# Second mixer's attention: the values of a step right behind its transposes, both parts of the main work behind them

## The reference, cut to what matters

```
z = rms_norm(x) @ w_in                      # all inputs of the three branches and their gates
o_a = fox_attention(q, k, v, f) * silu(..)  # 4 heads, causal, with a decay
o_b = conformer_conv(..) * silu(..)         # 31 taps, layer norm, a 256x256 product
o_c = nsa_attention(..) * silu(..)          # 8 heads: compressed + selected + window
x = x + concat(o_a, o_b, o_c) @ w_out
```

## Time and profile before

| what | value |
|---|---|
| median of 3 runs | 1589.8 us (1589.47 to 1591.67) |
| the profiled execution, its time | 1590.37 us |
| the profiled execution, its span | 1588.6 us |
| PE busy | 1574.3 us, 99% |
| DVE busy | 947.5 us, 60% |
| ACT busy | 800.6 us, 50% |
| POOL busy | 167.7 us, 11% |
| mean granted TensorE clock | 0.999 |

### The profile page before, as it was taken

The page is one execution under the profiler, slowest core; times in us unless marked ns, Lnnn a source line. Parts: engine busy times, 40 slices in busy tenths (PEclk is TensorE's granted clock), DMA queues, the critical chain, the costliest instruction groups (busy, mean ns, idle before and its releaser), DMA issues.

```text
span 1588.6 us, 22788 instructions
## 1 busy us (share of the span) xinstructions
PE 1574.3 (99%) x8752; PEld 1358.2 (86%) x8752; DVE 947.5 (60%) x1432; ACT 800.6 (50%) x1350; POOL 167.7 (11%) x187
## 2 busy tenths in 40 slices
PE   9999999999999999999999999999999999999998
PEld 7888899988888888888889988888888888889896
DVE  5555474544765554655456544575554679777876
ACT  6444465455464444544455545445444547553753
POOL 0000032211300000000011212131000201010110
PEclk9999999999999999999999999999999999999999
DMA  7555455333455554655545443446555473246321
GB/s 259 206 211 203 152 198 182 125 143 138 165 176 188 193 184 161 211 184 181 192 155 204 140 159 120 146 148 211 201 207 202 148 248 109 87 146 217 132 92 61
DMA packets 76142, 269.60 MB, mean 170 GB/s; under 512 B 8448, under 2 KB 9728, under 8 KB 76032
## 3 DMA queue, kind: packets, MB, share of 16 engines
q1 hardware_dynamic: 75744, 267.35, 47.6%
q10 hardware_dynamic: 288, 0.79, 0.1%
HBM read 267.06 MB, written 1.05 MB: 169 GB/s over the span
## 4 chain that ended last, share of the span: by engine, by line
PE 95%; DVE 2%; ACT 1%; DMA 1%; issue 1%; POOL 0%; POOLq 0%; SPq 0%
PE bank L1483 26%; PE bank L1485 26%; PE bank L1484 26%; PE bank L1489 5%; PE bank L1632 2%; PE bank L1547 2%; PE bank L1551 2%; PE bank L1543 2%; PE bank L1749 1%; PE bank L1617 1%; DVE cv L2342 1%; PE bank L1608 1%; PE bank L1610 1%; DVE wlo L2345 1%; PE bank L1721 0%
## 5 line engine op out<-in xcount | busy, mean ns | idle before, releaser
L2345 DVE TENSOR_TENSOR wlo<-raw,whi 128x1024 fp32r<-128x1024 f32 (+4 forms) x468 | 567.2, 1221 | 399.7 <-ACT whi L2031 370.1
L2031 ACT ACTIVATE whi<-raw 128x1024 fp32r<-128x1024 f32 (+4 forms) x496 | 508.1, 1036 | 407.6 <-PE bank L1485 383.7
L1483 PE MATMUL bank<-whi,hh 128*128 128x512 f32 (+3 forms) x1120 | 434.0, 387 | 0.0
L1485 PE MATMUL bank<-whi,hl 128*128 128x512 f32 (+3 forms) x1120 | 425.4, 380 | 0.0
L1484 PE MATMUL bank<-wlo,hh 128*128 128x512 f32 (+3 forms) x1120 | 424.7, 379 | 0.0
L1485 PEld LDWEIGHTS bank<-whi,hl 128*128 128x128 f32 x1120 | 210.6, 188 | 39.7
L1483 PEld LDWEIGHTS bank<-whi,hh 128*128 128x128 f32 x1120 | 210.8, 188 | 37.6 <-DVE ktm L2448 0.3
L1484 PEld LDWEIGHTS bank<-wlo,hh 128*128 128x128 f32 x1120 | 210.9, 188 | 37.3
L1483 PE MATMUL bank<-hh,whi 128*128 128x256 f32 x480 | 142.4, 297 | 1.0 <-DVE wlo L2345 1.0
L1483 PE MATMUL bank<-whi,gh 128*128 128x512 f32 x352 | 139.3, 396 | 0.0
L1485 PE MATMUL bank<-whi,gl 128*128 128x512 f32 x352 | 137.9, 392 | 0.0
(11 more groups left out here) (331 smaller groups left out, 1886.7 us busy)
## 6 DMA issues: line engine op xcount, KB each, us to landing
raw<-W SPq DMA_DIRECT2D x459, 512.0 KB, 3.2
whole<-W SPq DMA_DIRECT2D x16, 512.0 KB, 5.5
raw<-W SPq DMA_DIRECT2D x10, 384.0 KB, 2.9
raw<-W SPq DMA_DIRECT2D x8, 416.0 KB, 2.9
tab<-tab SPq DMA_DIRECT2D x6, 384.0 KB, 3.9
raw<-W SPq DMA_DIRECT2D x4, 426.0 KB, 3.2
raw<-W SPq DMA_DIRECT2D x6, 192.0 KB, 2.8
x<-x_in SPq DMA_DIRECT2D x2, 512.0 KB, 6.6
```

The costliest lines, as they stand in the source:

```text
L1483: e.matmul(dst, ah, bh, start=start, stop=False)
L1485: return e.matmul(dst, al, bh, start=False, stop=stop)
L2031: return e.activation(dst, src, ACT.Copy)
L2345: return e.tensor_tensor(dst, src, hi.bitcast(F), ALU.subtract)
```

## The change

The transposes of unit i-2 and the values of unit i-3 are issued one right behind the other. Tick b, which stood between them, is issued behind the values, just ahead of tick c. The number of ticks stays, and the split of the first `if` in two changes nothing.

```diff
@@ -1151,12 +1151,13 @@
             if i < n:
                 at_pair.append(next(todo))
                 scores(at_pair[i])
+            if i < n:
                 tick()
             if 0 <= i - 2 < n:
                 turn(at_pair[i - 2])
-            tick()
             if 0 <= i - 3 < n:
                 values(at_pair[i - 3])
+            tick()
             tick()
             yield
         self.kept = 0
```

## The result

The changed kernel takes 1595.02 us (median of 11 runs, 1592.88 to 1597.96), the one before 1591.21 us in the same rounds (11 runs, 1589.36 to 1592.95). The ratio is 1.0027 with a 95% interval [1.0019, 1.0035]: slower, and the low end of the interval is about the 0.2% that can be told from no change. The forecast said 3.2 us more. Measured are 3.8 us between the medians, 4.3 by the ratio.

The account below looks back on a forecast made before the run. PE, busy 99% of the span, was taken to bound the kernel. First layer 1.5 us and second 1.7 made 3.2 more, so 1593.0 us; range 1590.0 to 1595.2, the likeliest case's own range 1592.0 to 1594.3.

Parts of the forecast that it names:

- the four waits for ACT `wk`: PE's transposes waiting for ACT's copy that frees bank 5: 3.3 us in all, claimed to stay as before.
- Neighbours on PE: Joined pairs in 12 steps: 0.08 us paid per pair, slightly less regained at scores; taken as nothing, bounds -0.8 to +1.0.
- Step 8: Two small transposes of the compressed branch go behind the values: 0.1 us off each layer, bounds nothing and 0.2.
- The second rival: At the 12 joined pairs, hidden weight loads leave nothing to pay before the values: 0.8 us less, 1592.2; chance 0.08.
- Steps 6 to 8 of the second layer: A product DVE waits for ends 0.44 us later; 0.22 is covered, 0.22 us is new wait for transposes of unit 6.
- The predicted fifth row of the table: Sign in PE's table of waits: second layer's step 8 transposes wait 0.2 us for ACT `wk`, beside the four before.
- Steps 18 to 20: `fox_out` moves to tick a of step 19; waits of 0.66 and 0.94 us make 1.6 per layer, 3.2 in all.
- The first wait: In step 19, PE's transposes of `fox_out` wait for DVE's gates: 0.66 us in each layer.
- 6.6 and not 5.0: Sign: us from the scores of unit 19 to the first output matmul, changed kernel against before.
- The third rival: Second layer's step 5 wait of 2.48 us swallows the first layer's 1.5 us: 1591.5, or 1589.8 without the waits; chance 0.17.
- The fourth: DVE's and ACT's work before `m2_pw` comes late; PE waits about 1 us more in each layer: 1595.0; chance 0.15.
- The fifth: Joined pairs save slow starts, 1.8 us, plus 0.2 at step 8, with no waits in step 19: 1587.8; chance 0.08.

Follow-up runs that it names:

- e1: The changed kernel with the transposes of `fox_out` held one tick more, so they fall behind the values of unit 16 again: 1591.24 us, ratio 0.9999.
- e4: The changed kernel with the compressed values asked for ahead of `fox_out` and the layer norm behind it: 1595.6 us, ratio 1.0028.
- e2: The kernel before, nothing joined, with only the transposes of `fox_out` one tick sooner: 1595.31 us, ratio 1.0028.
- e3: The changed kernel with the layer norm's side generator asked ahead of that of `fox_out`: 1592.4 us, ratio 1.0006.

## Why the prediction was nearly right, and where it failed

- **What bounds the kernel, and that the four waits for ACT `wk` stay**: right. PE has 99% again, and the table keeps them. Two readings beside it were off. The four waits are not almost all that PE loses to named waits: PE's table of waits before names 4.3 us more in eight other rows, none above 1.0. Seven of them stand in the table of after unchanged; the eighth, 0.9 us for `x_in` at the start of the program, is gone there and belongs to the start, ahead of all that was changed. And PE's busy time, which should not have moved, grew by 3.0 us: part is the spell (e1, with one spell and neither wait, has 1575.7), part the matmul records behind a wait, which are longer (1.10 us and not 1.02 for the values). The starts of steps 0 to 6 of the first layer kept their distances to 0.01 us; that of step 7 is 0.08 late.
- **Neighbours on PE, costed at nothing**: right. Over its 6 pairs and step 8 the first layer gained 0.06 us, of which step 8 is 0.08; the bounds for all 12 pairs were -0.8 and +1.0. Both halves of the trade show: 0.43 to 0.44 us from four transposes to values (1333.45 to 1333.88, timeline of PE after), and scores that follow main work take 0.82 again (1331.19 to 1332.01).

```profile
1331.19 0.39 PE L1722 MATMUL bank<-kTh,qTh 128*128 128x512 f32 x1
...
1332.01 0.28 PE L1484 MATMUL bank<-hh,whi 128*128 128x256 f32 x1
...
1333.45 0.60 PE L1490 MATMUL bank<-kc,wk 128*128 128x128 f32 x4
1333.88 0.56 PE L1750 MATMUL bank<-ntm,wk 128*128 128x64 f32 x4
1334.37 0.33 PE L1490 MATMUL bank<-kc,hidr 64*128 64x64 f32 x2
1334.63 0.39 PE L1484 MATMUL bank<-hh,whi 128*128 128x256 f32 x1
```

- **Step 8, -0.1 us**: 1.18 us from the first of these groups to the main work (1333.45 to 1334.63), against 1.26. So -0.08, right.
- **The second rival, weight loads hidden**: fell. The 0.08 us in front of the values stayed at every joined pair outside the spell: 0.44 us where it was 0.36, 0.49 where it was 0.41, 0.22 where it was 0.14. The Trainium skill, "TensorE: Matmul & The Clock Gate", section "Step-by-step: what each phase is for", has the next weights pulled ahead of matmuls in flight; this trace doesn't show it hiding the change from transposes to values.
- **Steps 6 to 8 of the second layer, +0.22**: about 0.25, in the way that was forecast. Pairs, step 8 and this wait came to +0.19 in the second layer, pairs and step 8 alone to -0.06 in the first. DVE's read waits 0.87 us for PE and not 0.44, ACT's `fqh` 0.66 for DVE and not 0.23, and the transposes of unit 6 start right behind ACT's copy (timeline of all engines, after). The predicted fifth row of the table didn't come: the idle time stands at the weight load only. Up to the next start the loss can be seen.

```profile
1494.51 0.69 DVE L2343 SCALAR_TENSOR_TENSOR rgn<-bank,rsb 128x512 f32<-128x512 f32 x1 [0.87 <-PE bank L1486]
...
1495.23 0.63 ACT L2032 ACTIVATE fqh<-rgn 128x512 fp32r<-128x512 f32 x1 [0.66 <-DVE rgn L2343]
...
1499.25 0.38 ACT L2032 ACTIVATE wk<-bank 128x256 f32<-128x256 f32 x1
...
1499.68 0.42 PEld L1490 LDWEIGHTS bank<-kc,wk 128*128 128x128 f32 x4 [0.25 <-ACT wk L2032]
1499.69 0.66 PE L1490 MATMUL bank<-kc,wk 128*128 128x128 f32 x4
```

- **Steps 18 to 20, 1.60 us a layer**: right. The step-19 scores start 1.16 us later than before (1385.16 to 1386.32), by what came earlier. Add that to the prediction's times: `fqh` 1389.39 (measured 1389.38), end of `fql` 1390.72 (1390.69), values 1390.77 (1390.75). The first wait is 0.75 by starts and not 0.66, since the hand-over took 0.15 us (1387.82 to 1387.97) and not 0.05. The second is 0.79 and not 0.94, and the row says 0.63: the chain has one end, as e4 shows, so what the first wait and the work behind it take more, the second takes less. Together they make the values 1.58 us late (4.43 and not 2.85 from the scores). The named figure "6.6 and not 5.0" wasn't met as written: with 0.90 for the scores, 1387.22 to 1393.49 is 6.27. The output block behind took 3.19 us instead of 2.88, as in e1, which has neither wait; from its end the 1.60 is complete.
- **The third rival, given back**: fell, by e1 against the changed kernel.
- **The fourth, the convolution late**: fell. `m2_pw` starts without a wait. DVE's `ysl` ends at 1395.31, and PE comes at 1397.93: the slack grew from 1.7 us to 2.6.

```profile
1394.62 0.69 DVE L2346 TENSOR_TENSOR ysl<-cv,ysh 128x512 fp32r<-128x512 f32 x1 [0.70 <-ACT ysh L2032]
...
1397.93 0.36 PE L1484 MATMUL bank<-ysh,whi 128*128 128x256 f32 x1
```

- **The fifth, faster**: fell. The gates came when row 1385.80 said. e1, which is the change without the waits, isn't faster than before.

**The step that failed is the sum: it has no term for TensorE's granted clock, and the side was chosen on it as it stood.** The mechanism was right, and so was each term, to 0.1 us. In the table above the rows of the reordered steps add up to 3.4 us (1.60 + 1.62 - 0.06 + 0.2) against 3.2, and at equal clock the runs differ by 3.3 to 3.5. But 3.2 us is the very line between no change and slower, and I put the likeliest case, 0.47 against 0.45, on the lower side. On a line, small terms decide, and the clock was put at nothing without a reason, though the three runs before already lay from 1589.47 to 1591.67.

What the runs showed in its place: a spell costs 1.4 to 1.7 us, and the kernels with the waits show slightly more of them. Averaged over the runs of each kernel, the mean clock is 0.99745, 0.99740 and 0.99729 for after, e2 and e4, against 0.99786, 0.99818 and 0.99800 for before, e1 and e3. By 1.5 us for 0.001 that is some 0.6 us between before and after, an estimate, and 3.4 + 0.6 = 4.0 lies between the measured 3.8 and 4.3. For before and after alone the difference in clock is hardly larger than its own standard error. That the waits cause more spells is suggested by these counts and not shown; the spell in the profile of after lies at 1367 us, ahead of both waits, and can't come from them. So what makes the last 0.6 us stays open.

The time itself, 1593.0, was 2.0 us too low. Of that 0.6 is the term above, and 1.4 is the base: the median of three runs was 1589.8, while a usual run of the kernel before has one spell, and the medians of 11, 21 and 29 runs are 1591.21, 1591.38 and 1590.93. The base moves both kernels' times and not their difference. That 1595.02 still lies within 1590.0 to 1595.2 is luck: the upper end stood for the fourth rival, which didn't come, and the forecast's own range ended at 1594.3.

## What to carry to other kernels

When a move changes only the order on the bounding engine, look for the helper (here a side generator) that is keyed to an event of the moved work: here the event came a tick early and took `fox_out` with it, and holding it one tick took the whole cost back. Two waits that hang on one shared buffer are one chain; find its last hand-over, and price the buffer rather than the waits. Where the forecast lies on the edge of what can be measured, say which small unpriced terms there are and in which direction they act, before choosing a side.

## What the runs showed of the hardware that I had not expected

TensorE's granted clock falls to half for a short spell while PE is busy all the time: it is 0.66 on average over 1365 to 1370 in the changed kernel, with PE busy 5.00 of 5.00 us there and in the five us ahead. Ahead of this one PE had done the 24 small matmuls of the compressed scores up to 1364.10, then scores and a few values. The same work went at full clock in both executions of the kernel before, and in e1, e2 and e4. Each spell cost about 1.5 us and gave the runs of one kernel their steps of 1.4 to 1.7 us. What sets one off stays open. Three of the nine spells come right at or behind a wait of PE (near 1490 in e2 and e4, behind step 5's, and near 1557 in e4, behind step 19's); the others stand where PE has no gap. In e4's windows from 1550 to 1560 PE is busy for 8.58 of 10 us.

The idle time that the profile puts down to a wait is less than what the wait costs. Transposes to values took 1.23 us by starts (1389.52 to 1390.75) where 0.44 is usual, a loss of 0.79, and the row says 0.63.
